# Two transformer blocks on one core: the residual stream held transposed, three norms applied to results instead of inputs, the last sum formed in PSUM

## What is computed

```
# block 1
h  = rms_norm(x, norm1_g);  merged = gated sum of window attention, hyena and differential attention of h
x  = x + merged @ w_out
h2 = rms_norm(x, norm2_g)
x  = x + (silu(h2 @ ffn_w1) * (h2 @ ffn_w3)) @ ffn_w2
# block 2
h  = rmsnorm(x, attn_norm_g)          # then fox attention (8 heads) and stick-breaking attention (8 heads) of h
x  = x + concat(rmsnorm(o_fox), rmsnorm(o_sb)) @ w_out
h  = rmsnorm(x, ffn_norm_g)
u  = causal_dwconv(h @ w_up)          # three taps along the tokens, plus a bias
x  = x + (silu(u[:, :2816]) * u[:, 2816:]) @ w_down
return rmsnorm(x, final_norm_g)
# rms_norm(x, g) = x * rsqrt(mean(x*x) + 1e-6) * g, the mean over a token's features
```

## Time and profile before

| | us |
|---|---|
| median of 3 runs (1728.58 to 1731.97) | 1731.5 |
| the profiled execution, its own time | 1728.6 |
| its span, first to last instruction | 1726.8 |
| PE / DVE / ACT / POOL busy | 1648.0 / 833.2 / 658.0 / 271.0 |
| mean granted TensorE clock | 0.989 of full speed |

### The profile page before, as it was taken

One profiled execution on the slowest core, in us unless ns is written; L12 is line 12 of the kernel. 1 busy time (PEld: TensorE's weight loads), 2 busy tenths in 40 slices (PEclk: granted clock), 3 DMA queues, 4 the chain that ended last, 5 costly groups with the idle time before them and its releaser, 6 DMA issues.

```text
span 1726.8 us, 19076 instructions
## 1 busy us (share of the span) xinstructions
PE 1648.0 (95%) x7552; PEld 1301.6 (75%) x7552; DVE 833.2 (48%) x1332; ACT 658.0 (38%) x1150; POOL 271.0 (16%) x280
## 2 busy tenths in 40 slices
PE   5999998999999999999999998898999999999997
PEld 3566787767766787888888886676678788888886
DVE  5446455366356464333332224376663465556323
ACT  4332223454444433333222223366563344444221
POOL 3443205462012111000000002023200100000001
PEclk9999999999999999999999999999999999999999
DMA  6111112211121332333332321221102233233332
GB/s 227 56 67 47 49 49 85 80 50 62 61 62 49 110 98 73 98 98 98 98 98 98 97 87 63 93 69 42 50 13 74 74 97 98 95 94 92 111 98 72
DMA packets 39221, 139.51 MB, mean 81 GB/s; under 512 B 4331, under 2 KB 4971, under 8 KB 38940
## 3 DMA queue, kind: packets, MB, share of 16 engines
q1 hardware_dynamic: 39132, 138.29, 25.0%
HBM read 136.14 MB, written 2.10 MB: 80 GB/s over the span
## 4 chain that ended last, share of the span: by engine, by line
PE 84%; DVE 7%; POOL 4%; ACT 3%; issue 2%; DMA 1%; SPq 0%; DVEq 0%; POOLq 0%; ACTq 0%
PE ps L350 80%; PE ps L353 3%; DVE raw L970 1%; ACT whi L1357 1%; POOL small L1817 1%; POOL st L1881 1%; POOL small L1811 0%; DVE wlo L785 0%; ACT junk L1369 0%; DMA x<-in_x 0%; POOL small L1814 0%; DVE st L1057 0%; DVE xs L796 0%; DVE W L1199 0%; DVE olo L1162 0%
## 5 line engine op out<-in xcount | busy, mean ns | idle before, releaser
L785 DVE TENSOR_TENSOR wlo<-wraw,whi 128x1024 fp32r<-128x1024 f32 (+2 forms) x220 | 267.0, 1214 | 527.3 <-ACT whi L1357 527.1
L350 PE MATMUL ps<-hThi,whi 128*128 128x512 f32 x1128 | 453.6, 402 | 2.2 <-DVE hTlo L801 1.4
L1357 ACT ACTIVATE whi<-wraw 128x1024 fp32r<-128x1024 f32 (+2 forms) x244 | 253.0, 1038 | 511.6 <-PE ps L350 506.0
L350 PE MATMUL ps<-hThi,wlo 128*128 128x512 f32 x1128 | 441.0, 391 | 0.0
L350 PE MATMUL ps<-hTlo,whi 128*128 128x512 f32 x1128 | 440.9, 391 | 0.0
L350 PEld LDWEIGHTS ps<-hThi,whi 128*128 128x128 f32 x1128 | 212.7, 189 | 57.4 <-issue 15.7
L350 PEld LDWEIGHTS ps<-hThi,wlo 128*128 128x128 f32 x1128 | 212.6, 189 | 45.4
L350 PEld LDWEIGHTS ps<-hTlo,whi 128*128 128x128 f32 x1128 | 212.8, 189 | 44.5 <-issue 2.9
L350 PE MATMUL ps<-whi,achi 128*128 128x512 f32 x352 | 136.9, 389 | 0.0
L350 PE MATMUL ps<-wlo,achi 128*128 128x512 f32 x352 | 136.9, 389 | 0.0
L350 PE MATMUL ps<-whi,aclo 128*128 128x512 f32 x352 | 136.9, 389 | 0.0
(11 more groups left out here) (272 smaller groups left out, 2151.0 us busy)
## 6 DMA issues: line engine op xcount, KB each, us to landing
wraw<-in_ws SPq DMA_DIRECT2D x236, 512.0 KB, 3.5
x<-in_x SPq DMA_DIRECT2D x4, 512.0 KB, 7.8
x<-in_x SPq DMA_DIRECT2D x1, 2048.0 KB, 8.4
out<-xs SPq DMA_DIRECT2D x8, 256.0 KB, 2.0
dec<-in_dec SPq DMA_DIRECT2D x1, 1024.0 KB, 15.9
wraw<-in_ws SPq DMA_DIRECT2D x4, 256.0 KB, 2.6
vec<-in_vec SPq DMA_DIRECT2D x1, 788.0 KB, 4.9
w<-in_w SPq DMA_DIRECT2D x1, 512.0 KB, 14.3
```

The lines of the kernel that those rows point to most:

```text
L350: return t.matmul(o, l, r, start=first, stop=last)
L785: v.tensor_tensor(wlo[h][:, 0:width(i)], wraw[h][:, 0:width(i)], whi[h][:, 0:width(i)].bitcast(F32), ALU.subtract).then_inc(lo_done[h], 1)
L1357: a.activation(whi[h][:, 0:width(i)], wraw[h][:, 0:width(i)], ACT.Copy).then_inc(hi_done[h], 1)
```

## The change

The residual is turned once, while bC runs: `x` is loaded into another place and earlier (SP waits for the last scores of the differential heads, then loads it ahead of slot 66), PE transposes 32 blocks beside bC0 and bC1, ACT copies them to `xT`, features on the partitions. wo, dn and xo become "feat" groups; DVE adds each bank to `xT`, ACT writes gain x xT in rounded form, DVE the low part, and the next group takes these unnormed numbers. POOL squares the eight feature blocks and adds them up. Two slots into the next group PE sums over the partitions with a column of ones, DVE takes the mean, POOL the power -1/2, and POOL multiplies it into an identity, [128, 4 x 128]; one slot later PE multiplies that by ones, which puts the roots of all 512 tokens on every partition, and DVE copies this to R1 or R2. Results are multiplied by R1 or R2 (or by a column where tokens stand on the partitions: sv, fv): in up DVE for the gates, then ACT's SiLU in SBUF, then POOL multiplies by R1 again for the values' sake; in vp DVE for every bank, before all taps. xo's two groups of four slots become xs0, xs1 (the stick-breaking half of the rows, two slots each) and xf0, xf1 on top of them in the same banks. vd stays "tok"; PE adds x into its banks by products of `xT` with the identity at slot 1, ACT squares out of PSUM, and the output rows are made from PSUM: the first half first times `fg`, later scaled by ACT.

```diff
-            ("bC1", 4, 512, "feat"), ("wo0", 8, 512, "tok"), ("wo1", 8, 512, "tok")]
+            ("bC1", 4, 512, "feat"), ("wo0", 8, 512, "feat"), ("wo1", 8, 512, "feat")]
...
# tensor_program: norm() for n > 0 is gone
+        def x_turned():
+            w.wait_ge(in_res, 16)
+            for k in range(8):
+                bank = 4 + k % 4
+                take(bank)
+                for i in range(4):
+                    op = across(bank, i, x[:, i, k * 128:(k + 1) * 128])
+                op.then_inc(xT_tr, 1)
...
+        def token_squares(n, bank):
+            w.wait_ge(p_acc, 17 * n - 1)
+            take(bank)
+            for i in range(4):
+                op = mm(ps[bank][:, i:i + 1], sqs[:, i * 128:(i + 1) * 128], ones[:, 0:1], True, True)
+            op.then_inc(q_mm, 1)
...
+        def spread_roots(n, bank):
+            w.wait_ge(p_acc, 17 * n + 1)
+            take(bank)
+            mm(ps[bank][:], ones[:], sqt[:], True, True).then_inc(q_mm, 1)
...
+        flow.beside.append(x_turned())
         for half in range(2):
             group("bC%d" % half, ...
-                  lambda b: (b_v, 16 + 4 * half + b + 1))
-        residual("wo%d", 0, hT, lambda k, b: w.wait_ge(m_lo, k + 1))
-        norm(1, xs, 2)
+                  lambda b: (b_v, 16 + 4 * half + b + 1), 2)
+        flow.drain()
+        residual("wo%d", 1, lambda k: (mhi[:, k, :], mlo[:, k, :]), lambda k, b: w.wait_ge(m_lo, k + 1))
+        flow.later(2, lambda: token_squares(1, 0))
+        flow.later(3, lambda: spread_roots(1, 1))
...
-        residual("xo%d", 2, lambda k: (ohi[:, k, :], olo[:, k, :]),
-                 lambda k, b: w.wait_ge(o_lo, {3: 1, 0: 2, 2: 3, 1: 4}[b] + (0 if k < 4 else 4)))
-        norm(3, xs, 2)
+        for half in range(2):
+            group("xs%d" % half, lambda k: (ohi[:, k, :], olo[:, k, :]), lambda k, b: w.wait_ge(o_lo, 4), lambda b: None,
+                  last=False)
+        residual("xf%d", 3, lambda k: (ohi[:, 4 + k, :], olo[:, 4 + k, :]), lambda k, b: w.wait_ge(o_lo, 8), more=True)
...
+            def x_back(b, bank):
+                for k in range(4):
+                    mm(ps[bank][:, k * 128:(k + 1) * 128], xT[:, 4 * half + k, b * 128:(b + 1) * 128], ident, False, False)
+            group("vd%d" % half, lambda k: (achi[:, k, :], aclo[:, k, :]), lambda k, b: w.wait_ge(u_lo, 22 + k + 1),
+                  lambda b: None, beside=x_back)
# vector_program
+            def low(f):
+                w.wait_ge(e_hi, 8 * (n - 1) + f + 1)
+                v.scalar_tensor_tensor(hTlo[:, f, :], xT[:, f, :], col(gain, f), hThi[:, f, :].bitcast(F32), ALU.mult,
+                                       ALU.subtract).then_inc(e_lo, 1)
...
+                    v.tensor_tensor(xT[:, f, :], p[:], xT[:, f, :], ALU.add).then_inc(e_x, 1)
+                    if f:
+                        low(f - 1)
...
                 def conved(b, p, done):
-                    c, dst = f + 22 * (b // 2), ft[i]
+                    c, dst, t = f + 22 * (b // 2), ft[i], vt[q % 4]
+                    w.wait_ge(blocks, done)
+                    w.wait_ge(r_row, 6)
...
+                    v.tensor_tensor(t[:], p[:], R1[:], ALU.mult).then_inc(u_g, 1)
                     w.wait_ge(v_a, q + 1)
-                    v.scalar_tensor_tensor(dst[:, 1:S], p[:, 0:S - 1], col("cw2", 44 + c), dst[:, 1:S], ALU.mult,
+                    v.scalar_tensor_tensor(dst[:, 1:S], t[:, 0:S - 1], col("cw2", 44 + c), dst[:, 1:S], ALU.mult,
                                            ALU.add).then_inc(v_v, 1)
# scalar_program
                 def conved(b, p, done):
-                    w.wait_ge(blocks, done)
+                    w.wait_ge(u_g, 22 + q + 1)
...
-                    a.activation(ft[i][:], p[:], ACT.Identity, bias=col("cb2", c), scale=col("cw2", 88 + c)).then_inc(v_a, 1)
+                    a.activation(ft[i][:], vt[q % 4][:], ACT.Identity, bias=col("cb2", c), scale=col("cw2", 88 + c)).then_inc(v_a, 1)
# gpsimd_program
+                    g.tensor_tensor(sqt[:], xT[:, f, :], xT[:, f, :], ALU.mult).then_inc(p_acc, 1)
+                    w.wait_ge(p_acc, 17 * n - 16 + 2 * f)
+                    g.tensor_tensor(sqs[:], sqs[:], sqt[:], ALU.add).then_inc(p_acc, 1)
...
+        def spread(n):
+            w.wait_ge(r_row, 2 * n - 1)
+            g.tensor_tensor(small[:, 8:12], small[:, 12:16], col("mhalf", 0, 4), ALU.pow).then_inc(p_acc, 1)
...
+                    g.tensor_tensor(t[:], t[:], R1[:], ALU.mult).then_inc(u_sr, 1)
...
+                        g.tensor_tensor(dst[0:64, h, :], dst[0:64, h, :], R2[0:64, :], ALU.mult).then_inc(h_p, 1)
# sync_program
-        w.wait_ge(c_pv, 16)
+        weights(24, 66)
+        w.wait_ge(c_qk, 32)
         s.dma_start(x[:], x_dram).then_inc(in_res, 16)
...
-        w.wait_ge(n_sq, 24)
-        s.dma_start(mk[:], d["mask2"]).then_inc(in_mk, 16)
+        w.wait_ge(p_acc, 35)
+        s.dma_start(mk[:], d["mask2"]).then_inc(in_mask, 16)
```

More of the change, by code:

```diff
@@ L353, in across, with group @@
             return t.transpose(ps[b][:, c * 128:(c + 1) * 128], src, ident)
-        def group(name, act, ready, freed, rate=1):
-            first, n_s, n, mode = TABLE[name]
+        def group(name, act, ready, freed, rate=1, more=False, beside=None, last=True):
+            first, n_s, n, mode = PLACE[name]
             for s, b, end in slots(flow, name, rate, nothing):
@@ L361, in group @@
                     w.wait_ge(lo_done[h], i // HL + 1)
-                if s == 0:
+                if s == 0 and not more:
                     take(bank)
+                if s == 1 and beside:
+                    beside(b, bank)
                 for kk in range(2):
@@ L599, in differential, with residual @@
                 yield
-        def residual(names, n, act, ready):
+        def residual(names, n, act, ready, **more):
             for half in range(2):
-                group(names % half, act, ready, lambda b: (res, 8 * n + 4 * half + b + 1))
+                group(names % half, act, ready, lambda b: (e_x, 8 * (n - 1) + 4 * half + b + 1), **more)
         def out_norm_turn(q, bank):
@@ L1284, in vector_program @@
         for i in range(4):
-            scaled(0, i, x1, x1)
+            scaled(i)
         split(LA)
-        norm(0, "g1")
+        norm()
         flow.beside += [filters(), hyena()]
@@ L1314, in vector_program @@
         flow.drain()
+        flow.beside.append(iter(range(8)))
         for half in range(2):
-            group("bC%d" % half, branch(2, half))
-        residual("wo%d", 0, lambda i: scaled(1, i, xs, x))
-        norm(1, "g2")
-        ffn("up", 1)
-        residual("dn%d", 1, lambda i: scaled(2, i, xs, x))
-        norm(2, "g3")
-        group("sq", none)
-        group("sk", none)
+            group("bC%d" % half, branch(2, half), 2)
+        flow.drain()
+        residual("wo%d", 1, "g2")
+        flow.later(2, lambda: means(1, 0))
+        flow.later(3, lambda: roots(1, 1, R1))
+        ffn("up", 1)
+        residual("dn%d", 2, "g3")
+        flow.later(2, lambda: means(2, 4))
+        flow.later(3, lambda: roots(2, 5, R2))
+        group("sq", scores_out(sqT, 0.125))
+        group("sk", scores_out(skT, 1.0))
         group("fl", forget)
@@ L2015, in gpsimd_program @@
         flow.drain()
+        flow.beside.append(iter(range(8)))
         for half in range(2):
-            group("bC%d" % half, branch(2, half))
-        residual("wo%d", 0)
+            group("bC%d" % half, branch(2, half), 2)
+        flow.drain()
+        residual("wo%d", 1)
+        flow.later(2, lambda: spread(1))
         for j in range(11):
-            group("up%d" % j, none)
+            group("up%d" % j, gates(j))
         flow.flush()
-        residual("dn%d", 1)
+        residual("dn%d", 2)
+        flow.later(2, lambda: spread(2))
         group("sq", none)
@@ L2033, in gpsimd_program @@
         flow.drain()
-        residual("xo%d", 2)
+        for half in range(2):
+            group("xs%d" % half, none)
+        residual("xf%d", 3)
+        flow.later(2, lambda: spread(3))
         for j in range(11):
@@ L2037, in gpsimd_program, with last_roots @@
         flow.flush()
-        residual("vd%d", 3)
+        def last_roots(b):
+            w.wait_ge(n_rs, 16 + 2 * b + 1)
+            g.tensor_tensor(small[:, 8 + b:9 + b], small[:, 4 + b:5 + b], col("mhalf"), ALU.pow).then_inc(n_rs, 1)
+        group("vd0", none)
+        group("vd1", last_roots)
     def sync_program(s):
```

421 lines of the change are left out of this document (264 added, 157 removed).

## The result

| | before | after |
|---|---|---|
| median (7 runs each, same chip) | 1729.18 us | 1734.83 us |
| spread | 1726.42 to 1731.97 | 1732.07 to 1736.33 |
| profiled execution, its span | 1728.6, 1726.8 | 1735.6, 1733.7 |
| PE / DVE / ACT / POOL busy | 1648 / 833 / 658 / 271 | 1650.5 / 887.0 / 647.1 / 368.7 |

The ratio is 1.0029 (95% interval 1.0018 to 1.0040): slower by 5 us, a little more than the 0.2% that a measurement can tell. The forecast was 1.8 us faster. Against the profiled execution it was made from, 8.7 us of span are missing: 6.9 more, where 1.8 less was forecast.

The account below looks back on a forecast made before the run. TensorE, busy 1648 of 1726.8 us, was taken as the bound. 33.2 + 1.0 - 3.5 - 5.7 - 7.2 - 16.0 = 1.8 us gained, from 1731.5 to 1729.7; range 1720 to 1741, the forecast's own 1728 to 1735.

Parts of the forecast that it names:

- The seams: TensorE's gaps between wo, dn, xo and the group after each: all three close, 33.2 us gained.
- x turned: 32 transposes of x in 8 parcels between bC's products, 0.44 us each: 3.5 us paid on TensorE.
- the norms' sums: Per norm, four one-column products and one fp32 product spreading the roots on TensorE: 3 x 1.91 = 5.7 us paid.
- x put back: x added in the last product by 8 parcels of four fp32 products, 0.90 us each: 7.2 us paid.
- The seam's helpers: POOL's squares and sums end 8.3 us after the seam, before PE asks at 10.9: covered, 0 us.
- the rival with contention: POOL's squares and VectorE's low parts slow each other; POOL ends 12.2 us after the seam: 1736.7 us, chance 0.14.
- a sign of being wrong: PE waiting on POOL's sums after the second slot of up0, sq or vp0 would count against the forecast.
- The convolved group: In vp, VectorE alternating with ScalarE takes 2.97 us a block, delaying the weight split: 10 x 1.6 = 16.0 us lost.
- one of 256 us: Sign of being right: the stage given as 256 us grows to about 272, at clock 1.00.
- The second attention part: From sq to xo, scaling, forget chain, POOL's head products and xo in two parts: net 0, from -4 to +4 us.
- The case of the earlier trace: A two-operand SBUF instruction of VectorE, 0.68 us alone, took 2.88 beside a POOL one of 2.51.
- The end: Last chain loses an add and a row product, but ScalarE alternates square and copy: 1 us gained, between 0 and 1.4.

Follow-up runs that it names:

- The taps: Changed kernel with VectorE's two taps of a block in the convolved group moved behind the next block's multiply: 1713.55 us, ratio 0.9908.
- the tails runs: Changed kernel with both tails of a convolved group (SiLU, product, its split) put off one slot end on VectorE and ScalarE: 1716.13 us, ratio 0.9923.

## Why the prediction was wrong

*The seams (33.2).* Right: 9.0, 13.7 and 10.8 with the products behind them; the last is 1.3 better than the step, since a wait of 1.02 on the last head's low part in xo, with its late product, went too.

*x turned, the norms' sums, x put back.* x turned cost 3.7 for 3.5: bC took 25.5 us for 21.8, in every run of the changed code (the 3.3 of the table has the varying start in it). A sum with its roots was 1.9 in the step and 2.2 in up, 2.6 in vp (waits for POOL of 0.2 to 0.6 us in front; 1.8 where there is no wait). x_back: the parcels, and the product behind each, in the timeline of PE:

```profile
1603.69 1.05 PE L386 MATMUL ps<-vec,xT 128*128 128x128 f32 x8
1604.50 0.48 PE L386 MATMUL ps<-whi,achi 128*128 128x512 f32 x1
1604.81 0.40 PE L386 MATMUL ps<-wlo,achi 128*128 128x512 f32 x1
```

0.81, and the product behind it is 0.1 late: 0.90 as in the step. The stage up to PE's last product grew by 7.6 us for its 7.2.

*The seam's helpers, 0.* Nearly right by luck. POOL's end was put 8.3 us behind the seam and came at 11.2, 11.2 and 11.6; the rival with contention had said 12.2. PE asks at 10.9 to 11.0, so it waited 0.2, 0.2 and 0.6: the waits that the prediction had named as a sign of being wrong. The mechanism of that rival was there, its price at the seams was small: 1.8 us for all three, by the run in which ScalarE squares.

*The convolved group, 16.0: the mechanism right, the term mis-sized.* The wait stands where it was put, ten times, at the third slot. A block took 3.02 us for the 2.97 of the sum; ScalarE's Identity, which now reads SBUF, took 0.815 us for 0.781. By the Trainium skill's *VectorE: DVE Perf Modes*, "The TRN2 errata — SBUF-src ops pay a fixed extra latency per instruction", ScalarE pays 224 cycles from SBUF for 172 from PSUM: the trace agrees in direction. The prediction had used that section for VectorE and not for ScalarE. VectorE's side of the rule, eight steps shorter by 62 cycles, was not seen (0.750 from SBUF, 0.74 from PSUM).

The step had 1.6 us a pause, and a pause cost 1.97: 2.10 us lie between two products that are 0.23 apart otherwise, and the next is 0.10 late. The split was ready at 1468.25 (1467.02 + 1.23), where PE would have started its product at 1466.43 (1466.20 + 0.23): 1.82 late, 0.2 more than in the sum, which is the 0.05 of four blocks. The other 0.15 is the start behind the split (0.05) and the late next product (0.10), which the sum didn't have. The recorded wait of 1.71 counts from the modelled end of the product before, so it isn't the price either. Nine times 1.97 and once, at the first, 1.90: 19.6, 3.6 over the sum. The clock stayed at 1.00, as expected. The taps and the tails runs both gave the pauses back in full (20.2 us of vp). The stage that the prediction's last paragraph calls one of 256 us is vp with 240.4 us before and 262.3 after.

*The second attention part, net 0 from -4 to +4: the step that failed.* It came out at 4.2 above its share, outside that range. sv gained 2.3: the wait for the mask fell from 4.14 to 3.25 us, and the slow clock behind it from 6.8 to 3.4. sq and sk were within 1. fq and fk lost 5.5, and leaving out POOL's head multiplies gave 5.1 back. The step had counted them as work that fits between POOL's additions. It left out that a chain passes through the addition behind them, that VectorE's scan doubles beside them (2.02 for 0.96), and that short pauses here bring PE to 1.2 GHz: of the 5.5 us only 2.5 are waits. For the pauses in vp it had reasoned from the earlier trace rows that the clock holds through waits under 3 us. It held there, and not in fq, fk, where the kernel before already shows slow products behind waits of 1.67 and 1.05 (above). The case of the earlier trace rows had shown the contention, and the prediction used it at the seams, where there was room, and not here, where there was none.

*The end, 1.0 gained.* From PE's last product to the end of the span it was 9.1 us and is 8.4.

*The sum.* 3.6 in vp's pauses, 1.4 in the rest of vp (0.7 at the sum with its roots, 0.7 not placed), 4.2 in the attention part, 0.7 in vd and the end, 0.3 in up, less 1.3 at xo and 0.2 before wo: 8.7. A decisive term 18% too low and one term set at 0 in a range of 8 us turned a small gain into a small loss. Either error alone, 5.0 in vp or 4.2 in the attention part, would have left a loss of 2 to 3 us, which a measurement can't tell from nothing. That 1734.83 lies within the forecast's own range of 1728 to 1735 is luck: the sum started from the median of three runs, 1731.5, where seven give 1729.18, and the change went the other way.

## What to carry to other kernels

Two engines that hand a block back and forth, each in program order, cost the sum of their steps per block though neither is full: issue the next block's first step before waiting for the partner, or move the work that PE needs ahead of the group; here either was worth 20 us, and with four small edits more the changed kernel is 1.4% faster than the one before. Before counting a helper on POOL as free, look for a chain that is queued behind it and for two-operand work of VectorE beside it. Price a pause of PE from the spacing of its products, not from the recorded wait, count a parcel in the same way on both sides of a comparison, and judge edits of a few us by stages, since gains at neighbouring places need not add.

## What the runs showed of the hardware

- A wait of 1.71 us recorded on PE took 1.97 us out of the row of products, at nine of ten places (1.64 and 1.90 at the first).
- The granted clock stayed at 1.00 through ten pauses of 1.7 us in vp, with PE busy in full between them; in fq, fk, with products of 64 to 384 columns, parcels and more waits between, a pause of 2.24 and one of 1.67 followed by one of 1.06 were each followed by products 0.42 us apart. The same pair of waits was followed by 6.8 us at 1.2 GHz, by 3.4 or by none in kernels that differ a little.
- VectorE's low part of 0.75 us took 0.74 to 1.76 beside POOL's squares; POOL's addition of 1.28 took up to 2.2 there. A scan of 384 columns went from 0.96 to 2.02 beside POOL's multiply, one of 128 columns from 0.42 to 1.32, and a pair of those multiplies took 2.5 to 3.8.
- Four transposes of fp32 that start a bank, with products added on top, took 0.45 us, four fp32 products with the identity 0.90, each with the delay of the next product.
